# 112 candidate sums in the expert routing, and two half-size subtractions on GpSimd for each low part of the u weights

## The reference, cut to what matters

```python
def peer(h, w_q, sub_keys, u_tab, v_tab):
    ...
    s = jnp.einsum('thcd,hcnd->thcn', q, sub_keys)      # 8 heads, 2 halves, 128 keys
    sv, si = lax.top_k(s, PEER_TOPK)                    # PEER_TOPK = 16
    cand = (sv[:, :, 0, :, None] + sv[:, :, 1, None, :]).reshape(b * n, PEER_HEADS, PEER_TOPK * PEER_TOPK)
    score, pos = lax.top_k(cand, PEER_TOPK)
    i1 = jnp.take_along_axis(si[:, :, 0], pos // PEER_TOPK, axis=-1)
    i2 = jnp.take_along_axis(si[:, :, 1], pos % PEER_TOPK, axis=-1)
    expert = i1 * PEER_KEYS + i2
    gate = jax.nn.softmax(score.astype(jnp.float32), axis=-1).astype(h.dtype)
    ... # act = gelu(t . u_tab[expert]); out = sum(gate * act * v_tab[expert])
```

## Time and profile before

| | us |
|---|---|
| median of 3 runs | 3322.03 (3318.63 to 3327.59) |
| the profiled execution | 3330.15 |
| its span | 3328.3 |
| PE busy | 3179.4 (96%) |
| DVE busy | 2511.7 (75%) |
| ACT busy | 1465.8 (44%) |
| POOL busy | 1061.4 (32%) |

### The profile page before, as it was taken

One profiled execution on the slowest core, in us unless ns is written; L12 is line 12 of the kernel. 1 busy time (PEld: TensorE's weight loads), 2 busy tenths in 40 slices (PEclk: granted clock), 3 DMA queues, 4 the chain that ended last, 5 costly groups with the idle time before them and its releaser, 6 DMA issues.

```text
span 3328.3 us, 52861 instructions
## 1 busy us (share of the span) xinstructions
PE 3179.4 (96%) x20142; PEld 2921.5 (88%) x20142; DVE 2511.7 (75%) x4061; ACT 1465.8 (44%) x1864; POOL 1061.4 (32%) x706
## 2 busy tenths in 40 slices
PE   7999889999999999999999999999988999999999
PEld 5998689856777899999999999997868898989998
DVE  6877568686764489988749999897665797757777
ACT  5434344322443333366643333334234567864443
POOL 0110000010000278877673334451000698721110
PEclk9999899999999999999999999999999999999999
DMA  8984157461012267799999999994203578999996
GB/s 320 332 307 170 51 190 247 157 227 64 1 39 102 98 233 272 264 326 383 363 399 390 381 378 411 410 410 169 89 1 121 182 242 294 388 367 335 352 342 232
DMA packets 305610, 835.27 MB, mean 251 GB/s; under 512 B 22432, under 2 KB 185504, under 8 KB 254368
## 3 DMA queue, kind: packets, MB, share of 16 engines
q1 hardware_dynamic: 180096, 534.82, 44.2%
q0 software_dynamic: 67968, 247.49, 19.3%
q10 hardware_dynamic: 57376, 50.72, 4.5%
HBM read 750.10 MB, written 82.84 MB: 250 GB/s over the span
## 4 chain that ended last, share of the span: by engine, by line
PE 73%; DVE 13%; DMA 5%; ACT 3%; issue 2%; POOL 2%; SPq 1%; ACTq 0%; DVEq 0%; POOLq 0%
PE ps L3369 16%; PE ps L862 7%; PE ps L3352 6%; PE ps L1688 5%; PE ps L2909 5%; PE ps L873 4%; PE ps L2310 3%; PE ps L2933 3%; PE ps L3354 3%; PE ps L319 3%; DMA gates<-arena 3%; PE ps L2911 3%; PE ps L1430 2%; PE ps L1412 2%; DVE arena L2968 2%
## 5 line engine op out<-in xcount | busy, mean ns | idle before, releaser
L2883 POOL TENSOR_TENSOR arena_split<-ring,arena_split 128x1024 fp32r<-128x1024 f32 x228 | 569.5, 2512 | 886.5 <-ACT arena_split L2801 883.7
L2933 PE MATMUL ps<-xT_split,arena_split 128*128 128x384 f32 x2048 | 535.1, 337 | 4.0 <-ACT xT L2831 3.2
L3369 PE MATMUL ps<-arena_split 128*128 128x384 f32 x3072 | 532.7, 334 | 1.0 <-DVE arena_split L3292 1.0
L3369 PEld LDWEIGHTS ps<-arena_split 128*128 128x128 f32 x3072 | 532.4, 188 | 1.3 <-issue 1.3
L286 DVE TENSOR_TENSOR arena_split<-ring,arena_split 128x2048 fp32r<-128x2048 f32 x128 | 292.9, 2291 | 245.8 <-ACT arena_split L280 244.9
L3263 ACT ACTIVATE arena_split<-ring 128x2048 fp32r<-128x2048 f32 x126 | 241.7, 1918 | 504.3 <-PE ps L3369 314.7
L280 ACT ACTIVATE arena_split<-ring 128x2048 fp32r<-128x2048 f32 x128 | 244.4, 1915 | 378.3 <-PE ps L862 133.3
L2933 PEld LDWEIGHTS ps<-xT_split,arena_split 128*128 128x128 f32 x2048 | 372.1, 188 | 5.3 <-issue 4.2
L3289 DVE TENSOR_TENSOR arena_split<-ring,arena_split 128x2048 fp32r<-128x2048 f32 x128 | 293.3, 2291 | 98.9 <-ACT arena_split L3263 92.8
L557 POOL DMA_DIRECT2D arena<-in_side_weights x152 | 82.8, 546 | 824.2 <-DVE arena L577 288.5
L2909 PE MATMUL ps<-hT_split,arena_split 128*128 128x448 f32 x1024 | 338.7, 379 | 6.7 <-POOL arena_split L2883 4.5
(11 more groups left out here) (353 smaller groups left out, 6377.1 us busy)
## 6 DMA issues: line engine op xcount, KB each, us to landing
ring<-in_weights SPq DMA_DIRECT2D x396, 1024.0 KB
arena<-in_side_weights POOLq DMA_DIRECT2D x152, 512.0 KB
gates<-arena SPq DMA_DIRECT2D x76, 512.0 KB
arena<-gates SPq DMA_DIRECT2D x32, 768.0 KB
arena<-activations SPq DMA_DIRECT2D x64, 384.0 KB
activations<-xT ACTq DMA_DIRECT2D x128, 112.0 KB
arena<-gates SPq DMA_DIRECT2D x32, 448.0 KB
arena<-activations SPq DMA_DIRECT2D x64, 224.0 KB
```

Source lines behind the costliest of these rows:

```text
L2883: pool.tensor_tensor(low, self.raw(f)[:, j, :], high.bitcast(F32), ALU.subtract)\
L2933: mm = pe.matmul(k.ps[:, j, 0:self.T], self.u[:, 2 * (f % 2) + j, a, t * P:(t + 1) * P], self.h[b][:, t, :], start=n == 0, stop=n == 3 * D ...
L3369: mm = pe.matmul(k.ps[:, t, self.from_token:self.from_token + self.T], self.v[:, f % 2, a, j * D + t * P:j * D + (t + 1) * P], self.weight ...
```

## The change

`CANDIDATES = 112`: in place of all 256 sums of a head, VectorE forms two blocks, a < 4 with all 16 b (64 sums, at 0), and 4 <= a < 16 with b < 4 (48 sums, at 64). Every place with (a+1)(b+1) <= 16 is in one of them. The second `top` then runs on rows of 112. The place in a row has to be decoded by block: a is place >> 4 in the first block and (place >> 2) - 12 in the second, and the larger of the two is the right one in both; b is place & 15 or place & 3, by a mask.

On GpSimd each low part of 1024 elements per partition is made by two instructions of 512. The first of them waits as before, the second signals.

```diff
+BLOCKS = ((0, 4, 16, 0), (4, 16, 4, 64))
+CANDIDATES = 112
...
-        self.sums = k.room(next(at), PEER_HEADS, PEER_TOPK * PEER_TOPK)
+        self.sums = k.room(next(at), PEER_HEADS, CANDIDATES)
...
-                high, low = self.u[:, 2 * (f % 2) + j, 0, :], self.u[:, 2 * (f % 2) + j, 1, :]
-                pool.tensor_tensor(low, self.raw(f)[:, j, :], high.bitcast(F32), ALU.subtract)\
-                    .then_inc(k.chunk_products if j else self.u_low.sem, 1)
+                for half in range(2):
+                    mine = slice(half * D // 2, (half + 1) * D // 2)
+                    high, low = self.u[:, 2 * (f % 2) + j, 0, mine], self.u[:, 2 * (f % 2) + j, 1, mine]
+                    ins = pool.tensor_tensor(low, self.raw(f)[:, j, mine], high.bitcast(F32), ALU.subtract)
+                ins.then_inc(k.chunk_products if j else self.u_low.sem, 1)
...
-        sums = self.sums.rearrange("p h (a b) -> p h a b", b=t)
-        chain(dve.tensor_tensor(sums, v[:, :, 0, :].unsqueeze(3).to_broadcast([P, h, t, t]),
-                                v[:, :, 1, :].unsqueeze(2).to_broadcast([P, h, t, t]), ALU.add))
+        for lo, hi, n, at in BLOCKS:
+            sums = self.sums[:, :, at:at + (hi - lo) * n].rearrange("p h (a b) -> p h a b", b=n)
+            ins = dve.tensor_tensor(sums, v[:, :, 0, lo:hi].unsqueeze(3).to_broadcast([P, h, hi - lo, n]),
+                                    v[:, :, 1, 0:n].unsqueeze(2).to_broadcast([P, h, hi - lo, n]), ALU.add)
+        chain(ins)
...
-        dve.tensor_scalar(self.ia.bitcast(U32), self.si.bitcast(U32), 4, None, ALU.logical_shift_right)
-        chain(dve.tensor_scalar(self.ib.bitcast(U32), self.si.bitcast(U32), 15, None, ALU.bitwise_and))
-        dve.tensor_copy(self.ha, self.ia.bitcast(U32))
-        chain(dve.tensor_copy(self.hb, self.ib.bitcast(U32)))
+        place, by16, by4, mask = (x.bitcast(U32) for x in (self.si, self.ia, self.ib, self.fa))
+        dve.tensor_scalar(by16, place, 4, None, ALU.logical_shift_right)
+        dve.tensor_scalar(by4, place, 2, None, ALU.logical_shift_right)
+        chain(dve.tensor_scalar(mask, place, 64, 12, ALU.is_lt, ALU.mult))
+        dve.scalar_tensor_tensor(self.ha, by4, -12.0, by16, ALU.add, ALU.max)
+        chain(dve.scalar_tensor_tensor(self.fb.bitcast(U32), mask, 3, place, ALU.bitwise_or, ALU.bitwise_and))
+        chain(dve.tensor_copy(self.hb, self.fb.bitcast(U32)))
```

## The result

The changed kernel took 3330.72 us (median of 20 runs, 3325.35 to 3339.50), the kernel before 3323.74 us beside it (20 runs, 3318.22 to 3334.14). The ratio is 1.0020, with a 95% interval of 1.0012 to 1.0028: 7 us slower. The profiled execution took 3332.49 us, with a span of 3330.5 us.

The account below looks back on a forecast made before the run. TensorE was taken as the bound, with 9.0 us of waits nearly all that could be won. Terms -1.3 - 0.9 + 4.0 + 1.0 = +2.8 us on the 3322.0 us median gave about 3325 us, range 3310 to 3338.

Parts of the forecast that it names:

- The shorter searches: VectorE's routing: 112 instead of 256 sums saves net 6.7 us a tile, 27 us in layer 0, 13 in layer 1.
- Layer 0's turn and low parts, -1.3 and -0.9 us,: Layer 0: TensorE's waits at the turn (1.3 us) and for GpSimd's low parts (0.9 us) go away.
- The fixed cost d: GpSimd: extra time per half for splitting a subtraction in two, taken as 0.2 us, ends 0 and 0.37.
- the prediction's own formula: Layer 1: 58 halves times d, less 7.6 us, gives the time change; +4.0 us at d = 0.2.
- GpSimd as layer 1's pace: Layer 1's routing: full GpSimd delays TensorE, net +4.0 us; as slower rival 3336 us at d = 0.37, chance 0.18.
- the shorter waits of VectorE: Layer 1's routing: half-size pieces halve some twenty VectorE waits, roughly 22 us less, or nothing if VectorE misses the seam.
- rival (3): VectorE misses the seam between pieces; shorter searches suffice for both turns, time follows d alone; 0.66 together with the forecast.
- The term of -2.3 us at layer 1's turn: Layer 1: TensorE's 2.3 us wait at the turn disappears because VectorE is ready earlier.
- The gate stores, +1.0 us: Layer 0 with lots: gate stores come later behind SyncE's loads, five places at 0.2 us, +1.0 us (0 to +1.9).
- the two edits help one another: Routing: VectorE and GpSimd each hold up the other for an instruction's length, so shorter searches and halving belong together.

Follow-up runs that it names:

- the execution with the short wait: Third profiled execution of the changed kernel, nothing altered; its cast in layer 1's second tile lasted 4.47 us; 3327.92 us.
- the sums alone: Against the kernel before: only the 112 candidates, with whole GpSimd subtractions of 1024; 3321.74 us against 3324.80, ratio 0.9997.
- the experiment with the copies: 112 candidates, whole subtractions, layer 1's gate-weight copies moved behind the turn's last instruction; 3321.79 us against 3324.39 for the kernel before, ratio 0.9985.

## Why the prediction was right, and where its reasons were not

The time lay in the range, on the side that was forecast, and under the 10 us. That owes much to luck: +2.8 us were forecast and +7.0 measured, and most of the 7.0 comes from a wait that the sum has at nothing. The steps:

- **The shorter searches** held. A search over 112 took 259 to 269 ns on average, against about 267 named, and layer 0's VectorE time fell by 34.7 us in the stretch, with 27 forecast and shorter waits beside them.
- **Layer 0's turn and low parts, -1.3 and -0.9 us,** held: TensorE has no wait there, and the part is 2.9 us shorter.
- **The fixed cost d**, taken as 0.2 us with 0 and 0.37 as ends, is 2 x 1.25 - 2.35 = 0.15 us; whole subtractions started (2616.3 - 2606.9) / 4 = 2.35 us apart. The Trainium skill, "GPSIMD Engine Reference", section "Elementwise — side-by-side cycle accounting", had led to an estimate of 0.25; the measurement decides. With 0.15 the prediction's own formula gives 58 x 0.15 - 7.6 = +1.1 us for layer 1 and -0.1 in all. By it the kernel should have been at 3324, not at 3331. The agreement with 3325 owes something to a d that was too large.
- **GpSimd as layer 1's pace** was half right. In the execution with the short wait, TensorE waited 6.6 us for low parts, with 4.5 before, and the part was 2.8 us longer; +4.0 was forecast.
- **The step that failed is "the shorter waits of VectorE" with rival (3).** It said that missing the seam would cost nothing, because 13 us of shorter searches were far more than the turn needs. That priced a miss as one piece longer. A miss can be repeated at every seam until GpSimd has worked off its backlog, 25 to 30 times, and 30 us are more than the 13 saved and the slack there was. The prediction had both facts in front of it, that VectorE misses seams and that GpSimd would have no idle time left, and did not put them together.
- **The term of -2.3 us at layer 1's turn** was wrong as a gain. With the sums alone 1.9 us remain. The wait is not set by when the routing ends, but by VectorE's waits for subtractions between the Exp and the turn, as the experiment with the copies showed. In the changed kernel the wait is absent only because TensorE is late itself; in the execution with the short wait it was 2.6 us.
- **The gate stores, +1.0 us:** not to be seen. The part with lots was 4.3 us shorter, within what transfers scatter.

That the two edits help one another, as the prediction thought, is the opposite of what the runs show. The halving needs the shorter searches to hide it, and the shorter searches do better without it.

Of the shared access, the Trainium skill, "SBUF — State Buffer", section "SBUF: two separate sides", says that whichever starts first, a GpSimd operation or a VectorE operation in a two-port mode or with two SBUF inputs, has the shared pair for the whole instruction, and the other is fully blocked. The trace agrees, with 1.22 us and 2.3 us waits for pieces of 1.3 and 2.4 us. Nothing in that sentence says who is next, and the 37.00 us show that it need not be the one that waits.

What stays open is why a backlog keeps out that one instruction and not others. In the executions with 37.00 and with 4.47 us the cast came up at the same point of a piece, 0.72 us after its start, so the arrival within the piece doesn't tell them apart. Instructions that come right behind one that has just been let in got in at the next seam nearly always. The long waits were all of the first instruction after a search, but that is not enough either: the small addition behind the second search (line 2997) got in at the next seam all fourteen times in the same seven executions, with backlogs of 0.24 to 1.49 us. With pieces of 960 and 64 the cast got in while the backlog was still 1.14 us. What makes the backlog large or small when the cast comes up was not traced.

## What to carry to other kernels

Cutting a long instruction to shorten another engine's waits makes more seams, but it also fills the gaps between instructions, and a gap may be what lets the other engine in. Before such a cut, compare the pace that the cut engine will have with the pace of what feeds it: here 2.50 us against 2.63 left too little, where 2.35 left 0.23 us gaps. The price of a miss is then not the length of one instruction but the time that the cut engine needs to work off its backlog: here up to 1.97 us at 0.13 us a half. The backlog differs from execution to execution, so a profile of one execution may show either case.

## What the runs showed of the hardware that I had not expected

- VectorE was kept from its shared access through 25 to 30 GpSimd instructions in a row, 30.62 to 37.00 us, in five of seven profiled executions with 512-element pieces in layer 1 and no break (the others: 4.47 and 4.92 us in that tile), and for 15.75 us with pieces of 960 and 64. With whole subtractions no VectorE instruction beside them lasted over 5.6 us in layer 1. With 512-element pieces a wait ended when GpSimd's backlog was down to 0.08 to 0.18 us, twelve times of twelve.
- A GpSimd subtraction of 512 elements starts 1.25 us after the one before it, one of 1024 2.35 us: 0.15 us for the second instruction. With a wait for its own signal after every second piece it is 1.31 us.
- In the part between the layers, with the same instructions in every kernel, executions differed by up to 10 us (862.5 to 872.6).
- Behind a wait of 9.8 us TensorE's granted clock was 0.50 for about 6 us, and matmuls of 448 columns took 0.60 us in place of 0.37.
